# A fused two-block kernel on one core: product operands first in memory, modulations as rows, a second set of banks for the up products, and chains moved by a few ticks

## The chip, the cores and the metric

The kernel runs on one core of one Trainium2 chip. The metric is the time of one execution in microseconds on the device. The program on this core is five instruction streams, one for each engine: PE (TensorE, the matrix products), ACT (ScalarE, activations), DVE (VectorE, elementwise work), POOL (GpSimd) and SP (SyncE, which here only issues transfers). Each runs its own rows in order and meets the others at semaphores.

## The reference, cut to what matters

The reference runs two transformer blocks over 512 tokens of width 1024 (T = 4 tiles of 128 tokens), in float32. Block 1 is modulated by a vector c:

```python
ada = silu(c) @ w_ada + b_ada            # 6 groups of 1024: shift, gain, gate, twice
h = rmsnorm(x, n1) * (1 + gain1) + shift1
z = h @ w_in                             # q, k, v, index q and k, retention q, k, v, gate, ...
x = x + gate1 * (mix(sparse_attention(z), retention(z)) @ w_out)
h = rmsnorm(x, n2) * (1 + gain2) + shift2
x = x + gate2 * ((silu(h @ w_gate) * (h @ w_up)) @ w_down)     # 2816 wide
```

Block 2 has a rmsnorm, an attention with a compressed, a selected and a sliding branch (keys ks and kw, queries nq), a gated linear attention (decays from a small product gl, then exp and ln), and a feed-forward block whose two up products pass through a causal 3-tap convolution. The index scores choose the 256 keys that each query sees, so products have to be near full precision.

## The kernel before

**Products.** Every large product is made of three fp32r matmuls: an operand v is kept as a rounded high part and the rest, and hi·hi, hi·lo and lo·hi are added in one bank (`mm3`). A stationary operand of 128x128 meets up to 512 moving columns. The normed tokens lie in `Hh` and `Hl` (8 slices of 128 features by 512 tokens). Weights come in chunks of 128x1024 (512 KB) into `raw`, ACT writes their high part into `wh` (L1150), DVE the low part into `wl` (L1644). In the two down products, and in the projections after attention, the arrays `Ah` and `Al` serve too: as more places for weight chunks, or as the low and high part of the attention's output. `EH` and `EL` take the last slices of the second block's activation.

**Memory.** All arrays are allocated one after another in each partition, in the order of the allocation lines. Before, the order is X, Hh, Hl, raw, wh, wl, AR (a scratch arena), CST (tables), PRMT (parameters), BC, G, EH/EL (the same place as ACC), MC, ST, Ah/Al (the same place as AF). In bytes of a partition X begins at 16.5 KB, Hh and Hl lie at 33 to 66 KB, raw at 66 to 82, wh at 82 to 98, wl at 98 to 115, EH and EL at 199 to 207, and Ah and Al at 209 to 226.

**Order of the work.** `Weave` is a clock of ticks. A tick is the matmuls of one product step; all five programs walk through the same list of ticks. `w.after(n, f)` places f n ticks later in an engine's stream, `w.beside(generator)` advances a generator by one `yield` at each tick. Both only fix the place of small work between the dense matmuls in each engine's order; when it runs is left to the semaphores. `claim(b)` waits until the reader of PSUM bank b has freed it (there are 8).

**The start.** The stage iq multiplies the modulated, normed tokens with the index weights, feature slice by feature slice (k = 0 to 7). So slice k of the modulation has to be there before slice k of the product: silu(c) @ w_ada for 128 features of shift and 128 of gain. `LAND` takes the w_ada slices (1 MB each, 8 x 256 columns). DVE multiplies seven of eight row groups with silu(c) and adds them into two parts in G (`modulate`, L1659 and L1663); PE sums over the partitions with matmuls of one column (`modulation`, L526: CST,G and ST,AR). ACT then makes the modulated slice (L1204, L1205), DVE its low part. `norm_turn` is the transposes of the normed tokens (L535).

**The up products.** For a group j of 4 banks, the products of gate and up (m = 0 to 3) are made in banks 0 to 3, in each group the same four. ACT (silu, L1418) or, in block 2, ACT and DVE (the convolution, L1663) read them out. `down` uses all 8 banks for 4 tiles x 2 halves.

**The second attention.** In the stage 2nq, queries come tile by tile. Each tile's chain is: ACT copy and square, DVE head sums (L1666), POOL root, DVE scaling, gain and rotation (L1656), then the transposes on PE (`turn_heads`). `decays` makes the linear attention's decay factors beside it: 4 small products, DVE, then exp and ln on ACT (L1523, each with an ACT_TABLE_LOAD). `compressed` makes the compressed keys; it needs a gelu on ACT (L1488), whose result PE transposes. `attention` then runs score rows (DVE L1937), softmax, transposes and values between the product ticks. `linear` runs later, beside the output projection.

Of the kernel before, what the change touches and what calls it, by code (L numbers as in the profile page):

```python
# [114 lines left out]
NR, NH, NP = 4, 4, 8  # L115
# [194 lines left out]
def program(nc, x_in, cst_in, prm_in, bc_in, brow_in, wst, out):  # L310
# [12 lines left out]
    with ctx:  # L323
# [11 lines left out]
        wl = sb("wl", [P, NH, 1024], f32r)  # L335
        AR = sb("AR", [P, 13952])
# [4 lines left out]

        with nc.sbuf_tensor("EH", [P, 2, S], f32r) as EH, nc.sbuf_tensor("EL", [P, 2, S], f32r) as EL:
            pass
        ACC = sb("ACC", [P, 2, D])
        MC = sb("MC", [P, 32])
        ST = sb("ST", [P, 640])

        with nc.sbuf_tensor("Ah", [P, 4, S], f32r) as Ah, nc.sbuf_tensor("Al", [P, 4, S], f32r) as Al:
            pass
        AF = sb("AF", [P, 8, S])  # L350
# [57 lines left out]
        PART = [[G[:, 512 * i + 256 * j:512 * i + 256 * j + 256] for j in (0, 1)] for i in (0, 1)]  # L408
# [86 lines left out]

        TURNED = {"ks": (6, 4), "kw": (6, 3)}
# [19 lines left out]
        def tensor_program(e, on):  # L516
# [91 lines left out]
            def norm_turn(tag, t):  # L608
                xn, _ = norm_rows(tag, t)
                on.wait_ge(*dve.of((tag, "rows", t)))  # L610
                for n, b in enumerate(norm_banks(tag, t)):
# [4 lines left out]
                    free[b] = (act.of((tag, "gained", t)), dve.of((tag, "gained", t)))[n]  # L616

            on.wait_ge(s_cst, 16)
            for t in range(T):
                norm_turn("n1", t)  # L620

            def modulation(k):

                b, part, land = 6 + k % 2, PART[k % 2], LAND[k % 4]
                on.wait_ge(*act.of(("silu c",)))
                on.wait_ge(*dve.of(("sum", k)))
                claim(b)
                for m in (0, 1):
                    o = bank[b][:, m:m + 1]
                    mm(o, part[0][:, tok(m)], C("ones", 0, 1), True, False)  # L630
                    mm(o, part[1][:, tok(m)], C("ones", 0, 1), False, False)
                    x = mm(o, land[:, 7, tok(m)], SC[:, 7:8], False, True)
                x.then_inc(*small.mark(("modulation", k)))
                free[b] = dve.of(("mod1", k))

            modulation(0)
            modulation(1)

# [4 lines left out]
            for k, t in w.steps("iq"):  # L643
# [14 lines left out]
                else:  # L658
# [4 lines left out]
                    if k + 2 < 8:  # L663
                        modulation(k + 2)
# [183 lines left out]
            def up(prefix, tag, freed, fourth=None):  # L848
                for j, a, c in w.steps(prefix):
# [8 lines left out]
                    for m in (0, 2, 1, 3):  # L858
                        if c == 0 and a == 0:
                            claim(m)  # L860
# [1749 lines left out]
```

## Time and profile before

| what | value |
|---|---|
| median of 3 runs | 1628.5 us (1625.9 to 1630.48) |
| profiled execution | 1628.07 us, of which the span 1626.3 us |
| PE busy | 1590.8 us, 98% of the span |
| PE weight loads / DVE / ACT busy | 78% / 54% / 38% |
| mean granted TensorE clock | 0.994 |

PE is busy nearly all the time, so a gain has to come from PE's own time: idle stretches that are waits for another engine, matmuls that take longer than others of their kind, stretches at half clock, or small matmuls that fall away. "Busy" counts the modelled ends of matmuls, which overlap; two matmuls in a row that start 0.227 us apart are each listed with 0.39 us. What a matmul costs is therefore read from the distance between starts. In rows of the timeline the number in brackets is the idle time ahead of a row, and the engine and line that released it.

### The profile page before, as it was taken

Reading aid. Unit: us, or ns where it says so; the run is one execution under the profiler, and the core shown is the slowest. Engines: PE = TensorE matmul, PEld = TensorE weight load, DVE = VectorE, ACT = ScalarE, POOL = GpSimd, SP = SyncE. Lnnn points to the kernel's source line nnn. Section 1 sums busy time; section 2 is a strip of 40 time slices with the busy share of each in tenths; the row PEclk is TensorE's granted clock in tenths of the full one; section 3 lists DMA queues with packets and bytes.
Section 4 is the critical chain, followed back from the end, with each engine's and each line's share of the span. In section 5 each row is a group of like instructions: output and inputs, shape, how many; then the busy total and the mean of one; then the engine's idle time right before and its main releaser. Section 6 shows DMA issues by size and latency. Waiting matters only on the chain.

```text
span 1626.3 us, 19784 instructions
## 1 busy us (share of the span) xinstructions
PE 1590.8 (98%) x8003; PEld 1268.0 (78%) x8003; DVE 881.5 (54%) x1628; ACT 614.2 (38%) x1069; POOL 43.8 (3%) x82
## 2 busy tenths in 40 slices
PE   6999999999999999999999999899999999999999
PEld 5877877678888888888888886666768888887887
DVE  6769785655375653232333655676457455555432
ACT  4443334542312432222322454466425334344320
POOL 1000000000000000000000101100000000000000
PEclk8999999999999999999999999999999999999999
DMA  7512121136245334322222151110113222222221
GB/s 299 198 65 103 53 75 69 53 129 246 104 168 168 104 131 155 104 91 101 86 99 99 34 188 47 39 53 14 40 53 116 91 104 91 88 85 100 104 78 52
DMA packets 44883, 165.76 MB, mean 102 GB/s; under 512 B 5108, under 2 KB 5236, under 8 KB 43640
## 3 DMA queue, kind: packets, MB, share of 16 engines
q1 hardware_dynamic: 44792, 164.50, 28.8%
q8 instruction: 63, 1.03, 0.3%
q14 instruction: 28, 0.23, 0.0%
HBM read 162.38 MB, written 2.10 MB: 101 GB/s over the span
## 4 chain that ended last, share of the span: by engine, by line
PE 91%; DVE 4%; ACT 2%; issue 1%; POOL 1%; DMA 0%; SPq 0%; DVEq 0%; ACTq 0%
PE bank L526 87%; PE bank L535 4%; DVE AR L1656 1%; DVE AR L1663 1%; DMA X<-in_x 0%; DVE wl L1644 0%; POOL ST L2420 0%; DVE X L1656 0%; ACT wh L1150 0%; ACT AR L1161 0%; ACT AR L1173 0%; DVE CST L1656 0%; POOL ST L2418 0%; DVE ST L1666 0%; DVE Hl L1656 0%
## 5 line engine op out<-in xcount | busy, mean ns | idle before, releaser
L526 PE MATMUL bank<-wh,Hh 128*128 128x512 f32 (+1 forms) x1008 | 408.8, 406 | 0.4 <-DVE wl L1644 0.4
L526 PE MATMUL bank<-wh,Hl 128*128 128x512 f32 (+1 forms) x1008 | 392.6, 390 | 0.0
L526 PE MATMUL bank<-wl,Hh 128*128 128x512 f32 (+1 forms) x1008 | 392.2, 389 | 0.0
L1150 ACT ACTIVATE wh<-raw 128x1024 fp32r<-128x1024 f32 (+2 forms) x195 | 203.6, 1047 | 403.6 <-PE bank L526 391.4
L1644 DVE TENSOR_TENSOR wl<-raw,wh 128x1024 fp32r<-128x1024 f32 (+2 forms) x195 | 234.3, 1209 | 138.9 <-ACT wh L1150 138.3
L526 PEld LDWEIGHTS bank<-wh,Hh 128*128 128x128 f32 x1008 | 190.5, 189 | 58.0 <-issue 21.7
L526 PEld LDWEIGHTS bank<-wh,Hl 128*128 128x128 f32 x1008 | 190.2, 189 | 40.5
L526 PEld LDWEIGHTS bank<-wl,Hh 128*128 128x128 f32 x1008 | 190.7, 189 | 34.3
L526 PE MATMUL bank<-Hh,wh 128*128 128x512 f32 (+2 forms) x504 | 190.5, 378 | 2.6 <-DVE AR L1663 1.2
L526 PE MATMUL bank<-Hh,wl 128*128 128x512 f32 (+2 forms) x504 | 189.4, 376 | 0.0
L526 PE MATMUL bank<-Hl,wh 128*128 128x512 f32 (+2 forms) x504 | 189.3, 376 | 0.0
L526 PEld LDWEIGHTS bank<-Hh,wh 128*128 128x128 f32 (+1 forms) x504 | 94.5, 187 | 21.3 <-issue 1.6
L1656 DVE TENSOR_TENSOR Hl<-AR,Hh 128x512 fp32r<-128x512 f32 x68 | 45.8, 690 | 116.0 <-ACT Hh L1429 112.9
L526 PEld LDWEIGHTS bank<-Hl,wh 128*128 128x128 f32 (+1 forms) x504 | 94.5, 187 | 17.6 <-issue 0.2
L526 PEld LDWEIGHTS bank<-Hh,wl 128*128 128x128 f32 (+1 forms) x504 | 94.5, 187 | 17.7
L535 PE MATMUL bank<-CST,AR 128*128 128x128 f32 (+1 forms) x545 | 89.2, 285 | 18.7 <-DVE AR L1659 12.3
L535 PEld LDWEIGHTS bank<-CST,AR 128*128 128x128 f32 (+1 forms) x545 | 66.3, 144 | 52.1 <-issue 10.3
L526 PE MATMUL bank<-Hh,Ah 128*128 128x512 f32 (+1 forms) x272 | 100.5, 370 | 0.5 <-DVE X L1656 0.5
L526 PE MATMUL bank<-Hh,Al 128*128 128x512 f32 (+1 forms) x272 | 100.1, 368 | 0.0
L526 PE MATMUL bank<-Hl,Ah 128*128 128x512 f32 (+1 forms) x272 | 100.0, 368 | 0.0
L1150 ACT ACTIVATE Ah<-raw 128x1024 fp32r<-128x1024 f32 x46 | 48.5, 1057 | 129.7 <-PE bank L526 128.0
L1663 DVE SCALAR_TENSOR_TENSOR AR<-bank,PRMT,AR 128x511 f32<-128x511 f32 x88 | 63.9, 746 | 56.7 <-ACT AR L1624 55.1
(245 smaller groups left out, 1878.5 us busy)
## 6 DMA issues: line engine op xcount, KB each, us to landing
raw<-in_wst SPq DMA_DIRECT2D x268, 512.0 KB, 3.6
AR<-in_wst SPq DMA_DIRECT2D x8, 1024.0 KB, 6.5
X<-in_x SPq DMA_DIRECT2D x8, 512.0 KB, 4.9
AR<-in_wst SPq DMA_DIRECT2D x5, 512.0 KB, 6.0
out<-X SPq DMA_DIRECT2D x8, 256.0 KB, 2.1
CST<-in_cst SPq DMA_DIRECT2D x1, 1619.0 KB, 9.6
raw<-in_wst SPq DMA_DIRECT2D x4, 296.0 KB, 2.8
BC<-in_bc SPq DMA_DIRECT2D x2, 512.0 KB, 6.9
```

Source lines behind the costliest of these rows:

```text
L526: return e.matmul(o, l, r, start=start, stop=stop, skip_group_check=True)
L535: return e.transpose(o, a, C("ident")[0:n, 0:n])
L1150: e.activation(HI[slot[i]][:, 0:width(i)], raw[:, i % NR, 0:width(i)], ACT.Copy).then_inc(*w_hi.mark(i))
L1644: e.tensor_tensor(LO[slot[i]][:, 0:n], raw[:, i % NR, 0:n], HI[slot[i]][:, 0:n].bitcast(f32), SUB).then_inc(*w_lo.mark(i))
L1656: return e.tensor_tensor(o, a, b, op).then_inc(*dve.mark(*events))
L1663: return e.scalar_tensor_tensor(out=o, in0=a, scalar=s, in1=b, op0=op0, op1=op1).then_inc(*dve.mark(*events))
```

## The change

Four things are changed; nothing of what is computed.

- The allocation order becomes Hh, Hl, wh, wl, Ah/Al, EH/EL (with ACC), X, raw, AR, CST, PRMT, BC, G, MC, ST. Hh is then at 16.5 to 33 KB, Hl up to 49, wh up to 66, wl up to 82, Ah and Al at 82 to 98, EH and EL up to 107; X, raw, AR, CST, PRMT, BC, G and ST lie higher than before, up to 226 KB.
- Modulation slices are made differently. `SCZ` holds silu(c) as a stationary operand of 32 columns, of which the first is silu(c) and 31 are zero. `modulation_rows` streams the w_ada slice past it: 8 matmuls of 256 columns, four of them into each of four groups of 32 output rows. DVE copies the rows to SBUF (`MROW`), and `modulation_columns` sums them with 2 matmuls of one column. Slices 4, 6 and 7 (`ADDED`) are instead summed on DVE, all eight groups into one row. The x tiles come ahead of the first w_ada slice in SP's queue, both halves of the last token tile are copied out by ACT, and the full-precision slice (`FUL`) of slices 0 and 1 is made by DVE.
- `up_bank` puts group j's four products in banks 0 to 3 or 4 to 7 in turn, and the first down step takes tiles 2 and 3 first.
- In block 2, `decays` starts two ticks sooner on three engines, and waits correspondingly longer before its second part, whose banks alternate; the compressed keys use bank 7 for 6; the last two query tiles' scaling and transposes come later (10 and 13 or 14 ticks instead of 4 and 7); `linear` passes one tick between its sums and its scaling.

```diff
-        X = sb("X", [P, T, D])
         Hh = sb("Hh", [P, 8, S], f32r)
         Hl = sb("Hl", [P, 8, S], f32r)
-        raw = sb("raw", [P, NR, 1024])
         wh = sb("wh", [P, NH, 1024], f32r)
         wl = sb("wl", [P, NH, 1024], f32r)
+        with nc.sbuf_tensor("Ah", [P, 4, S], f32r) as Ah, nc.sbuf_tensor("Al", [P, 4, S], f32r) as Al:
+            pass
+        AF = sb("AF", [P, 8, S])
...
+        X = sb("X", [P, T, D])
+        raw = sb("raw", [P, NR, 1024])
         AR = sb("AR", [P, 13952])
...
+        ADDED = (4, 6, 7)
+        def mod_bank(k):
+            return 5 + k % 3 if k else 0
+        def up_bank(j, m):
+            return m + 4 * (j % 2)
...
+            def modulation_rows(k):
+                b = mod_bank(k)
+                on.wait_ge(*dve.of(("spread",)))
+                on.wait_ge(s_pre[k % 4], 16 * (k // 4 + 1))
                 claim(b)
+                for q in range(8):
+                    r = slice(32 * (q % 4), 32 * (q % 4) + 32)
+                    x = mm(bank[b][r, 0:256], SCZ[:, q, :], LAND[k % 4][:, q, :], q < 4, q >= 4)
+                x.then_inc(*small.mark(("mod rows", k)))
+            def modulation_columns(k):
+                b = mod_bank(k)
+                on.wait_ge(*dve.of(("mod rows", k)))
                 for m in (0, 1):
+                    x = mm(bank[b][:, 256 + m:257 + m], MROW[k % 2][:, tok(m)], C("ones", 0, 1), True, True)
...
                     if k + 2 < 8:
-                        modulation(k + 2)
+                        modulation_columns(k + 2)
+                if (k, t) == (0, 0):
+                    modulation_columns(1)
+                if t == 2 and k + 2 < 8 and k + 2 not in ADDED:
+                    modulation_rows(k + 2)
...
+                    tiles = ((2, 3, 0, 1) if k == 0 else range(T)) if t is None else (t,)
...
             def decays():
-                for _ in range(3):
-                    yield
+                yield
...
-                    lambda t: w.after(7, lambda: turn_heads("nq", t, 2, TN[t], dve.of(("nq", "roped", t)))), 2)
+                    lambda t: w.after((7, 7, 13, 14)[t], lambda: turn_heads("nq", t, 2, TN[t], dve.of(("nq", "roped", t)))), 2)
...
-                    w.after(2, root)
-                    w.after(4, scale)
+                    w.after((2, 2, 2, 4)[t], root)
+                    w.after((4, 4, 10, 10)[t], scale)
...
+                    yield
                     on.wait_ge(*pool.of(("lroot", t)))
...
+            load_x(0)
             e.dma_start(PRMT[:, 0:now], prm_in[:, 0:now]).then_inc(s_prm, 16)
             e.dma_start(CST[:, 0:early], cst_in[:, 0:early]).then_inc(s_cst, 16)
-            load_x(0)
-            load_x(1)
+            for t in range(1, T):
+                load_x(t)
             land(0)
-            load_x(2)
-            load_x(3)
```

**PE at the very start.** Before, PE's stream opens with the transposes of all four token tiles (32), then modulation slices 0 and 1, each as two triples of one-column matmuls (G holds DVE's sums, ST silu(c), AR the w_ada slice), then the dense matmuls.

```order
L535 MATMUL bank<-CST,AR 128x128 x32
L526 MATMUL bank<-CST,G 128x1 x2
L526 MATMUL bank<-ST,AR 128x1
L526 MATMUL bank<-CST,G 128x1 x2
L526 MATMUL bank<-ST,AR 128x1
L526 MATMUL bank<-CST,G 128x1 x2
L526 MATMUL bank<-ST,AR 128x1
L526 MATMUL bank<-CST,G 128x1 x2
L526 MATMUL bank<-ST,AR 128x1
L526 MATMUL bank<-wh,Hh 128x512
L526 MATMUL bank<-wl,Hh 128x512
```

After the change, the same place reads as follows (G is now the copied rows, ST the widened silu(c)).

```order
L548 MATMUL bank<-CST,AR 128x128 x24
L539 MATMUL bank<-AR,ST 32x256 x8
L548 MATMUL bank<-CST,AR 128x128 x8
L539 MATMUL bank<-CST,G 128x1 x2
L539 MATMUL bank<-AR,ST 32x256 x8
L539 MATMUL bank<-wh,Hh 128x512
L539 MATMUL bank<-wl,Hh 128x512
L539 MATMUL bank<-wh,Hl 128x512
L539 MATMUL bank<-CST,G 128x1 x2
L539 MATMUL bank<-wh,Hh 128x512
L539 MATMUL bank<-wl,Hh 128x512
L539 MATMUL bank<-wh,Hl 128x512
```

Eight transposes moved behind the first group of row matmuls, a second group stands ahead of the first dense matmul, slice 1's one-column matmuls moved behind three dense ones, and each slice has 2 of these where there were 6.

**ACT in the stage 2nq.** L1541 and L1543 are the copy and square of a query tile, L1523 exp and ln of the decays (with their table loads), L1463 copies of the kw keys' transposes, L1488 the gelu of the compressed keys. Before:

```order
L1541 ACTIVATE AR<-bank 128x512
L1543 ACTIVATE AR<-AR 128x512
L1541 ACTIVATE AR<-bank 128x512
L1543 ACTIVATE AR<-AR 128x512
L1523 ACT_TABLE_LOAD
L1523 ACTIVATE AR<-AR 128x256 x4
L1463 ACTIVATE AR<-bank 128x2x256 x2
L1523 ACT_TABLE_LOAD
L1523 ACTIVATE AR<-AR,CST 128x256 x4
L1488 ACT_TABLE_LOAD
L1488 ACTIVATE AR<-bank 128x256
```

After:

```order
L1572 ACTIVATE AR<-bank 128x512
L1574 ACTIVATE AR<-AR 128x512
L1552 ACT_TABLE_LOAD
L1552 ACTIVATE AR<-AR 128x256 x4
L1552 ACT_TABLE_LOAD
L1552 ACTIVATE AR<-AR,CST 128x256 x4
L1572 ACTIVATE AR<-bank 128x512
L1574 ACTIVATE AR<-AR 128x512
L1493 ACTIVATE AR<-bank 128x2x256 x2
L1518 ACT_TABLE_LOAD
L1518 ACTIVATE AR<-bank 128x256
```

The exp, the ln and their two table loads moved ahead of the second tile's copy and square; between the last of these and gelu only two key copies and the gelu's own table load are left.

**DVE around the first score rows of the second attention.** A score row is a pair of ISA rows. The chain of a query tile's scaling is the five rows from `AR<-AR,ST 128x512` to `AR<-ST 128x8x16`. Before, tile 2's chain stands ahead of the first score row, and tile 3's right behind it:

```order
L1656 TENSOR_TENSOR AR<-AR,ST 128x512
L1656 TENSOR_TENSOR AR<-AR,PRMT 128x512
L1656 TENSOR_TENSOR ST<-AR,CST 128x128
L1656 TENSOR_TENSOR ST<-AR,CST 128x8x8 x2
L1656 TENSOR_TENSOR AR<-ST 128x8x16
L1666 TENSOR_REDUCE ST<-AR 128x8
L1644 TENSOR_TENSOR wl<-raw,wh 128x1024
L1937 ISA AR,ST<-bank,CST 128x128
L1937 ISA ST 128x1
L1937 ISA AR,ST<-bank,CST 128x128
L1937 ISA ST 128x1
L1656 TENSOR_TENSOR AR<-AR,ST 128x512
```

After, no such chain stands there; tile 2's stands behind the fifth score row, ahead of the division for an earlier row's softmax:

```order
L2001 ISA AR,ST<-bank,CST 128x128
L2001 ISA ST 128x1
L2001 ISA AR,ST<-bank,CST 128x128
L2001 ISA ST 128x1
L1692 TENSOR_TENSOR AR<-AR,ST 128x512
L1692 TENSOR_TENSOR AR<-AR,PRMT 128x512
L1692 TENSOR_TENSOR ST<-AR,CST 128x128
L1692 TENSOR_TENSOR ST<-AR,CST 128x8x8 x2
L1692 TENSOR_TENSOR AR<-ST 128x8x16
L1708 RECIPROCAL ST<-ST 128x2
L1695 TENSOR_SCALAR AR<-AR,ST 128x128 x2
```

Each of the two chains moved behind several score rows; the rows of a chain are the same.

## Rows read from the trace of the kernel before

**Rows 1.** The page: busy time of each engine, share of the span, instructions.

```profile
PE 1590.8 (98%) x8003; PEld 1268.0 (78%) x8003; DVE 881.5 (54%) x1628; ACT 614.2 (38%) x1069; POOL 43.8 (3%) x82
```

**Rows 2.** Waits of PE by releaser: us in total, times, longest us.

```profile
PE bank L535 <- ACT AR L1488: 3.1, 1, 3.1
...
PE bank L526 <- DVE AR L1663: 2.5, 3, 1.3
...
PE bank L526 <- DVE ST L1937: 2.1, 2, 1.5
PE bank L535 <- DVE PRMT L1669: 1.8, 1, 1.8
...
PE bank L535 <- DVE AR L1656: 1.5, 1, 1.5
```

**Rows 3.** Timeline of PE, the start: start us, duration us, operation, records, idle before.

```profile
16.25 1.72 PE L535 MATMUL bank<-CST,AR 128*128 128x128 f32 x8 [0.42 <-DVE AR L1659]
...
23.40 1.01 PE L526 MATMUL bank<-CST,G 128*128 128x1 f32 x4 [2.88 <-DVE G L1663]
...
25.98 0.77 PE L526 MATMUL bank<-wh,Hh 128*128 128x512 f32 x1
...
31.46 0.50 PE L526 MATMUL bank<-CST,G 128*128 128x1 f32 x4
...
32.72 0.48 PE L526 MATMUL bank<-wh,Hh 128*128 128x512 f32 x1
```

**Rows 4.** Timeline of the start, ACT and DVE.

```profile
12.73 1.04 ACT L1161 ACTIVATE AR<-X 128x1024 f32<-128x1024 f32 x1
...
21.28 2.06 DVE L1663 SCALAR_TENSOR_TENSOR G<-AR,ST,G 128x256 f32<-128x256 f32 x5
```

**Rows 5.** Windows: stretch, us, PE busy (records), granted clock, DMA share, GB/s.

```profile
16.55:30.20 13.65, 10.77 (x42) 0.50 0.88 346
1003.00:1006.40 3.40, 2.84 (x8) 0.50 0.00 0
1033.70:1037.10 3.40, 3.40 (x14) 0.50 0.02 5
```

**Rows 6.** Timeline of PE in the first down product, Ah, then wh.

```profile
606.64 0.40 PE L526 MATMUL bank<-Hh,Ah 128*128 128x512 f32 x1
...
617.80 0.39 PE L526 MATMUL bank<-Hh,wh 128*128 128x512 f32 x1
...
628.00 0.39 PE L526 MATMUL bank<-Hh,wh 128*128 128x512 f32 x1
```

**Rows 7.** PE by line and shape: operands (moving, stationary), count, busy, mean, idle.

```profile
L526 PE MATMUL bank<-wh,Hh 128*128 128x512 f32 x976 | 398.3, 408 | 0.4 <-DVE wl L1644 0.4
...
L526 PE MATMUL bank<-Hh,wh 128*128 128x512 f32 x432 | 168.9, 391 | 1.6 <-DVE AR L1663 1.2 <-ACT AR L1418 0.4
...
L526 PE MATMUL bank<-Hh,Ah 128*128 128x512 f32 x208 | 82.2, 395 | 0.0
...
L526 PE MATMUL bank<-Ah,Hh 128*128 128x512 f32 x112 | 44.4, 397 | 0.0
...
L526 PE MATMUL bank<-wh,Ah 128*128 128x512 f32 x64 | 26.8, 418 | 0.0
```

**Rows 8.** Timeline of PE: two matmuls of 64 outputs each, the next.

```profile
996.87 0.65 PE L526 MATMUL bank<-AR,CST 128*64 128x256 f32 x4
997.46 0.50 PE L526 MATMUL bank<-wh,Hh 128*128 128x512 f32 x1
```

**Rows 9.** Timeline of ACT: the gelu of the compressed keys.

```profile
1003.12 0.38 ACT L1488 ACTIVATE AR<-bank 128x256 f32<-128x256 f32 x1
```

**Rows 10.** Timeline of DVE: a query tile's scaling, first and last step; the division.

```profile
1027.87 0.69 DVE L1656 TENSOR_TENSOR AR<-AR,ST 128x512 f32<-128x512 f32 x1 [1.46 <-POOL ST L2420]
...
1029.92 0.29 DVE L1656 TENSOR_TENSOR AR<-ST 128x128 f32<-128x128 f32 x1
...
1042.10 0.17 DVE L1672 RECIPROCAL ST<-ST 128x2 f32<-128x2 f32 x1 [0.66 <-ACT AR L1318]
```

More of the change, by code:

```diff
@@ L1017, in decays @@
                     yield
-                for _ in range(3):
+                for _ in range(5):
                     yield
@@ L1208, in scalar_program @@
                 norm_root("n1", t, (s_in[t], 16))
-                if t:
-                    rows_out(t - 1)
-            rows_out(T - 1)
+            for t in range(T):
+                if t == 3:
+                    split_high(place["iq", 0])
+                rows_out(t)
             split_high(place["ik", 0])
-            split_high(place["iq", 0])
             features(0)
@@ L1515, in decays @@
             def decays():
-                for _ in range(3):
-                    yield
+                yield
                 for t in range(T):
@@ L1632, in vector_program @@
         def vector_program(e, on):
+            early = set()
             def consume(i):
+                if i in early:
+                    return
+                early.add(i)
                 key, k, n = chunks[i][0], chunks[i][1], width(i)
@@ L1715, in modulated, with modulation_rows @@
-            def modulated(k):
-                b = bank[6 + k % 2]
-                on.wait_ge(*small.of(("modulation", k)))
-                tt(MC[:, k:k + 1], b[:, 0:1], W("b01", k, 1), ADD)
-                stt(MC[:, 8 + k:9 + k], b[:, 1:2], W("b01", 8 + k, 1), W("n1", k, 1), ADD, MUL, ("mod1", k))
+            def modulation_rows(k):
+                on.wait_ge(*small.of(("mod rows", k)))
+                if k >= 2:
+                    on.wait_ge(*small.of(("modulation", k - 2)))
+                copy(MROW[k % 2], bank[mod_bank(k)][:, 0:256], ("mod rows", k))
@@ new lines, in modulated, with modulation_sums @@
+            def modulated(k):
+                b = bank[mod_bank(k)]
+                on.wait_ge(*small.of(("modulation", k)))
+                tt(MC[:, k:k + 1], b[:, 256:257], W("b01", k, 1), ADD)
+                stt(MC[:, 8 + k:9 + k], b[:, 257:258], W("b01", 8 + k, 1), W("n1", k, 1), ADD, MUL, ("mod1", k))
+            def modulation_sums(k):
+                land, row = LAND[k % 4], MROW[k % 2]
+                on.wait_ge(s_pre[k % 4], 16 * (k // 4 + 1))
+                on.wait_ge(*small.of(("modulation", k - 2)))
+                ts(row, land[:, 0, :], SC[:, 0:1], None, MUL, None)
+                for q in range(1, 8):
+                    own()
+                    stt(row, land[:, q, :], SC[:, q:q + 1], row, MUL, ADD, *[("mod rows", k)] * (q == 7))
+                    if q in (1, 3, 5, 6, 7):
+                        yield
@@ L1721, in features_low, with added_rows, features @@
+            def added_rows():
+                for k, tick in zip(ADDED, (8, 16, 22)):
+                    while w.k < tick:
+                        yield
+                    yield from modulation_sums(k)
+            def features(k):
+                own()
+                on.wait_ge(*act.of(("n1", "gained", T - 1)))
+                ts(FUL[k % 2], AF[:, k, :], MC[:, 8 + k:9 + k], MC[:, k:k + 1], MUL, ADD)
             def features_low(k):
+                own()
                 on.wait_ge(*act.of(("n1", "high", k)))
@@ L1745, in vector_program @@
             ts(W("b01", 8, 8), W("b01", 8, 8), 1.0, None, ADD, None)
+            e.memset(SCZ, 0.0).then_inc(*dve.mark())
+            own()
+            on.wait_ge(*act.of(("silu c",)))
+            copy(SCZ[:, :, 0], SC, ("spread",))
             open_sum(2)
@@ L2245, in decays @@
             def decays():
-                for _ in range(3):
-                    yield
+                yield
                 for t in range(T):
@@ L2492, in sync_program @@
             for k in range(4):
-                on.wait_ge(*small.of(("modulation", k)))
+                on.wait_ge(*small.of(("mod rows", k)))
                 land(k + 4)
```

149 lines of the change are left out of this document (73 added, 76 removed).

## The prediction

> **What bounds the kernel now.** I read the busy times on the page first: PE is busy for 98% of the span, DVE for 54%, ACT for 38% [rows 1]. The reader is to see that no other engine can be the limit on average, and that all a change can win lies in PE's own stream. So the next views are those of PE: what it waits for [rows 2], the start [rows 3], the stretches at half clock [rows 5], and the distance between the starts of equal matmuls [rows 6]. Three kinds of loss come out of them.
>
> The start: the first dense matmul begins at 25.98 us [rows 3]. Ahead of it PE stands still for 2.88 us for DVE's modulation sums, and then spends 2.58 us (23.40 to 25.98) on slice 1's one-column matmuls.
>
> Waits in the stream: 3.1 us for the gelu, 1.8 and 2.1 us where the second attention opens, 1.5 us once in the output projection, and 2.5 us for PSUM banks of the up products [rows 2], with 0.4 us more for silu [rows 7]. Two of them are followed by a stretch of 3.4 us at a granted clock of 0.50, half of the full speed of 2.4 GHz; each comes after PE stood still [rows 5].
>
> A slow operand: in the first down product, 48 matmuls with a chunk in Ah and Al take from 606.64 to 617.80, 11.16 us or 232.5 ns each; the 45 after them, with a chunk in wh and wl, take until 628.00, 226.7 ns each [rows 6]. Work, shapes and clock are the same; what differs is where the operand lies (Ah and Al are above 209 KB, wh and wl at 82 to 115 KB).
>
> **The change part by part.** Sums are against the profiled execution, 1628.07 us (1.8 us around the span of 1626.3); the median of the runs is 0.4 us above it, which I leave out.
>
> *Memory.* Matmuls of 512 columns with an Ah or Al operand: 208, 112 and 64, each of three products, so 1152 [rows 7]. At 5.8 ns each that is 6.7 us, if the new place (82 to 98 KB) treats them as it treats wh, which lies in it today. Bounds: nothing, and 6.7 us. I take 6.7, since the same shapes run at 226.7 ns there. The small matmuls' operands (AR, CST, G, ST) and X go higher; no row shows them at two heights, and their effect I put at 0.
> The Trainium skill, "SBUF — State Buffer", section "SBUF: two separate sides", says that PE and ACT have ports of their own and never wait on anyone; it knows no dependence on the address. By that rule the memory part would give 0, which is rival 1. The 5.8 ns of this trace speak against it, but they show a difference, not its cause.
>
> *Start.* Before, the last x tile's square ran at 12.73 [rows 4], behind 1 MB of w_ada in the queue. At the 346 GB/s of [rows 5] that megabyte takes 3.0 us, so the last tile comes about 3 us sooner and the first w_ada slice lands about when the tile did, near 12.9. Then PE does the first group of row matmuls. The nearest row is a pair of matmuls with 256 columns in two groups of 64 outputs, 0.59 us from start to start [rows 8] (4 records, since a float32 matmul leaves two). Eight matmuls in four groups of 32: if four run side by side, two rounds, 1.2 us; if only two do, 2.4 us; if none does, 4.7 us. I take 1.6 us at full clock, nearer to the low end because the pair in rows 8 plainly shares its time, and 3.2 us at half clock, which this stretch has [rows 5]. 12.9 + 3.2 gives 16.1; the last tile's transposes follow (16.25 to about 17.7 before) and end at 17.7. The copies out, the gain, the slice's high and low part then take about what the idle stretch of 2.88 us held [rows 3]: first dense matmul at 20.6, so 5.4 us sooner. DVE's sums for a slice (five steps 2.06 us, [rows 4]) are gone from this path; slice 1's group of rows lies inside those 2.9 us. Bounds: 18.5 (LAND early, four at once) and 24.
>
> *In the stream of iq.* Before, six slices cost 1.26 us each (31.46 to 32.72, 12 records, [rows 3]), 7.6 us. After, seven have 4 such records, 0.42 us, 2.9 us together, and slices 2, 3 and 5 have a group of rows of 1.6 us, 4.8 us. Together 7.7 us: a loss of 0.1, with bounds of a gain of 1.1 (groups of 1.2) and a loss of 9.4 (groups of 4.7). Slices 4, 6 and 7 go to DVE, 8 steps of 0.41 us each (2.06 over five, [rows 4]), spread over three or more ticks each; they hide behind the dense matmuls. Without that cover each would delay one slice by some 3 us.
>
> *Banks.* The 2.5 us of waits for the convolution (three of them, [rows 2]) and 0.4 us for silu [rows 7] go, since a group's banks have been free for a whole group: 2.9 us. What is late next is nothing: between groups PE already runs at the even distance.
>
> *Second block.* (a) The gelu waited on ACT behind exp, ln and their table loads and ran at 1003.12 [rows 9]; PE had been idle for its result for 3.1 us [rows 2]. The order shows exp and ln ahead of the second tile's copy. They come two ticks (24 dense matmuls at 0.227 us) or 5.4 us sooner, and let a copy and a square in, about 1.2 us. Exp needs the logits, which PE and DVE make two ticks sooner as well. The gelu then comes near 999, before PE asks (near 1000.5): all of the 3.1 us. (b) The two stretches at half clock vanish with their waits: PE was busy 2.84 and 3.40 us in them, half of that is 3.1 us; I take 2.8, since the small matmuls in them gain less. (c) Where the second attention opens, waits of 2.1 us (two, for score rows) and 1.8 us (for a copy) stood behind the two tiles' scaling chains on DVE: all 3.9 us. (d) In `linear`, two DVE operations of about 0.6 us leave the chain that ended in a wait of 1.5 us: 1.2 us. (e) The two chains come back later. One is 2.34 us of DVE (1027.87 to 1030.21) and enters ahead of a division that had 0.66 us of idle time before it [rows 10]: each can hold back the softmax's division, and with it PE's transposes, by up to 1.7 us; at least by nothing, if PE asks later. I take 1.2 us each, 2.4 us. Sum: 3.1 + 2.8 + 3.9 + 1.2 - 2.4 = 8.6 us.
>
> **Sum.** 6.7 + 5.4 - 0.1 + 2.9 + 8.6 = 23.5 us; 1628.07 - 23.5 = 1604.6 us.
>
> **Rivals.**
>
> 1. *The place in memory is not the cause.* Ah and Al could be slow for what is written or read beside them. Against: rows 6 are one stage with one pattern, and all shapes with Ah show it. For: one example of each height. The part gives 0: 1611.3 us.
> 2. *Row matmuls run two at a time.* 0.8 us more for each of three groups in the stream, 1.6 us for each of two at the start at half clock: 5.6 us, 1610.2 us.
> 3. *The moved chains stall the attention.* Full 1.7 us each (1.0 us more), and PE's idle time there brings one stretch at half clock back (1.7 us) and a second wait behind it (1 us): 1608.3 us.
> 4. *The group of rows runs one matmul after another.* 3.1 us more for each of three, 6.2 us for each of two: 21.7 us, 1626.3 us, no change that can be told. The pair in rows 8 speaks against it.
> 5. *Slower.* The distance depends on the place in another way than by height, and the operands' new places (Hh, Hl, wh and wl all move) are ones where it is 232.5 ns. In this kernel 4224 matmuls of 512 columns have neither Ah nor Al (976 and 432 of two kinds, each of three products, [rows 7]). At 5.8 ns they lose 24.5 us, and the 6.7 us don't come: 1635.8 us. It decides from 4.0 ns each (16.8 us of other gains over 4224). Against it: Hl and wh go where Hh and Hl run evenly today; only the places of X and raw, which Hh and wl take, are untried.
>
> That the change doesn't do what it says is possible for the banks alone (a group's reader might be later than a whole group); it is worth at most 2.9 us and lies in the range.
>
> **How the numbers follow.** Chances: forecast 0.52 (its own range 1598 to 1609: the chains free of cost, 2.4, and a start at 18.5, 2.1, below; a start at 23 and chains at 1.7 above), rival 1 0.19, rival 2 0.10, rival 3 0.11, rival 4 0.04, rival 5 0.04. The first four lie below 1612; two of them together (1 and 2, 1617) are rare. Range: 1597 to 1615 us. A measurement of this kernel tells 0.3%, 4.9 us, from no change. Faster: 0.52 + 0.19 + 0.10 + 0.11 = 0.92; the same: 0.04 (rival 4); slower: 0.04 (rival 5).
>
> **What would show it.** Memory: the distance in the down product is 227 ns in every chunk. Start: the first dense matmul near 20.6; a group of row matmuls (16 records) takes 1.2 to 1.6 us at full clock. Banks: no wait of PE for L1418's or L1663's successors between groups. Second block: no wait for the gelu, no stretch at 0.50 behind 1000 us, and small waits of about 1.2 us for the division's result or for score rows further on in the attention. The prediction is wrong if dense matmuls run at 232 ns anywhere in a stage with no small work, if a group of rows takes over 2.5 us, or if new waits of PE add up to more than 5 us.

## The result, and the profile after

The changed kernel takes 1603.93 us (median of 4 runs, 1602.26 to 1605.5), against 1628.88 us for the kernel before (4 runs). The ratio is 0.9849, with a 95% interval of 0.9829 to 0.9868: 24.95 us faster. The prediction was 1604.6 us, with a range of 1597 to 1615. The profiled execution took 1602.26 us, with a span of 1600.4 us.

PE's line of the page (before: [rows 1]): PE is still busy for 98% of a shorter span, with 14.8 us less work.

```profile
PE 1576.0 (98%) x8019; PEld 1257.9 (79%) x8019; DVE 875.0 (55%) x1604; ACT 613.2 (38%) x1068; POOL 44.3 (3%) x82
```

**Where the time came from.** Both kernels issue the same 5976 dense matmuls in the same order, so the start of the same matmul in both timelines shows what has been gained up to there. Before, three of them:

```profile
51.92 0.47 PE L526 MATMUL bank<-wh,Hh 128*128 128x512 f32 x1
...
880.99 0.39 PE L526 MATMUL bank<-Ah,Hh 128*128 128x512 f32 x1
...
1229.94 0.40 PE L526 MATMUL bank<-wl,Hh 128*128 128x512 f32 x1
```

After, the same three:

```profile
43.07 0.47 PE L539 MATMUL bank<-wh,Hh 128*128 128x512 f32 x1
...
868.29 0.39 PE L539 MATMUL bank<-Ah,Hh 128*128 128x512 f32 x1
...
1210.59 0.39 PE L539 MATMUL bank<-wl,Hh 128*128 128x512 f32 x1
```

With the first dense matmul (25.98 in [rows 3], 18.71 below) and the two spans this gives the gain up to each place:

| up to | before | after | gained |
|---|---|---|---|
| first dense matmul | 25.98 | 18.71 | 7.3 |
| near the end of iq | 51.92 | 43.07 | 8.9 |
| down product of block 1, past its half | 880.99 | 868.29 | 12.7 |
| second attention and half of the output projection | 1229.94 | 1210.59 | 19.4 |
| end | 1626.3 | 1600.4 | 25.9 |

**The start** answers to [rows 3]. PE's timeline, with the idle time ahead of a row in brackets:

```profile
13.38 1.40 PE L539 MATMUL bank<-AR,ST 128*32 128x256 f32 x16
14.72 1.09 PE L548 MATMUL bank<-CST,AR 128*128 128x128 f32 x8
15.65 0.50 PE L539 MATMUL bank<-CST,G 128*128 128x1 f32 x4
16.64 1.07 PE L539 MATMUL bank<-AR,ST 128*32 128x256 f32 x16 [0.49 <-ACT AF L1223]
18.71 0.47 PE L539 MATMUL bank<-wh,Hh 128*128 128x512 f32 x1 [1.00 <-DVE Hl L1692]
19.01 0.39 PE L539 MATMUL bank<-wl,Hh 128*128 128x512 f32 x1
...
19.48 0.50 PE L539 MATMUL bank<-CST,G 128*128 128x1 f32 x4
...
21.40 1.07 PE L539 MATMUL bank<-AR,ST 128*32 128x256 f32 x16
22.40 0.50 PE L539 MATMUL bank<-wh,Hh 128*128 128x512 f32 x1
...
23.89 0.50 PE L539 MATMUL bank<-CST,G 128*128 128x1 f32 x4
24.26 0.48 PE L539 MATMUL bank<-wh,Hh 128*128 128x512 f32 x1
```

The 16 records of a group of row matmuls take 1.00 us from start to start (21.40 to 22.40) at full clock. That is less than the 1.2 us that two rounds of four would take by [rows 8], so the eight matmuls run four at a time. The second dense matmul starts 0.3 us after the first, and the two slices' one-column matmuls cost 0.36 and 0.37 us (19.48 to 19.84 and 23.89 to 24.26). The first dense matmul waited 1.00 us for DVE's low part. All of this ran at full clock: dense matmuls follow each other every 0.23 us, and the windows say the same (columns as in [rows 5]):

```profile
16.00:30.00 14.00, 12.51 (x95) 1.00 1.02 418
1014.00:1024.00 10.00, 9.90 (x59) 1.00 0.01 2
1028.20:1031.70 3.50, 3.50 (x16) 0.56 0.00 0
```

The third window holds a stretch at 0.50 (its mean is 0.56, since it reaches a little beyond the stretch), in the second attention, where PE never stood still for more than 0.42 us in the 14 us before it.

**An Ah chunk** answers to [rows 6]: 48 matmuls in 10.88 us, 226.7 ns each; then 45 in wh in 10.20 us, 226.7 ns each. One correction: the stretch at 606 us, which the heading of [rows 6], the prediction and the expectations call the first down product, belongs to the up products of block 1. ACT goes on reading their banks for silu until 804.80 us before the change, and the down product follows. Ah chunks serve in both stages, in the up products as the stationary and in the down products as the moving operand, and nothing else in the argument hangs on the name.

```profile
596.31 0.39 PE L539 MATMUL bank<-Hh,Ah 128*128 128x512 f32 x1
...
607.19 0.39 PE L539 MATMUL bank<-Hh,wh 128*128 128x512 f32 x1
...
617.39 0.39 PE L539 MATMUL bank<-Hh,wh 128*128 128x512 f32 x1
```

**Waits of PE** (columns as in [rows 2]). The convolution's and silu's waits are gone, the gelu's too. What took 2.5 us is new.

```profile
PE bank L539 <- DVE AR L1692: 3.4, 4, 1.1
PE bank L548 <- DVE AR L1705: 2.5, 1, 2.5
...
PE bank L539 <- DVE ST L2001: 0.2, 1, 0.2
...
PE bank L548 <- DVE AR L1692: 0.3, 1, 0.3
```

### The profile page after: what moved, and what is told of

It is laid out like the page before. It is cut to its first block, busy times and chain, and to the rows that moved or that the text cites. A ratio compares the mean times of both kernels' runs of the same rounds, so it can differ in the third digit from the quotient of the medians.

```text
span 1600.4 us, 19799 instructions
## 1 busy us (share of the span) xinstructions
PE 1576.0 (98%) x8019; PEld 1257.9 (79%) x8019; DVE 875.0 (55%) x1604; ACT 613.2 (38%) x1068; POOL 44.3 (3%) x82
## 4 chain that ended last, share of the span: by engine, by line
PE 92%; DVE 5%; ACT 2%; issue 1%; POOL 1%; DMA 0%; SPq 0%; DVEq 0%; ACTq 0%
PE bank L539 87%; PE bank L548 4%; DVE AR L1692 1%; DVE wl L1680 1%; POOL ST L2483 0%; DVE G L1699 0%; DVE X L1692 0%; DVE Hl L1692 0%; ACT wh L1176 0%; ACT AR L1199 0%; DVE CST L1692 0%; ACT AR L1187 0%; DMA CST<-in_cst 0%; DVE ST L1702 0%; DVE AR L1699 0%
## 5 line engine op out<-in xcount | busy, mean ns | idle before, releaser
L1176 ACT ACTIVATE wh<-raw 128x1024 fp32r<-128x1024 f32 (+1 forms) x195 | 203.6, 1047 | 398.2 <-PE bank L539 386.2
L1680 DVE TENSOR_TENSOR wl<-raw,wh 128x1024 fp32r<-128x1024 f32 (+1 forms) x195 | 234.2, 1208 | 137.1 <-ACT wh L1176 136.1
```

The source lines that it names most:

```text
L1176: e.activation(HI[slot[i]][:, 0:width(i)], raw[:, i % NR, 0:width(i)], ACT.Copy).then_inc(*w_hi.mark(i))
L1680: e.tensor_tensor(LO[slot[i]][:, 0:n], raw[:, i % NR, 0:n], HI[slot[i]][:, 0:n].bitcast(f32), SUB).then_inc(*w_lo.mark(i))
```

## The experiments

Each kernel was timed beside the kernel before on the same chip; its medians there were 1629.11, 1629.25 and 1628.54 us. Twelve kernels ran, in three groups. Where one is set against the changed kernel (1603.93 us), the two were timed on different occasions; those differences carry the spread of both, some 2 us. The traces allow a finer comparison, since the dense matmuls come in the same order in all fourteen kernels.

### One part at a time

Each of the first four is the kernel before with one part of the change.

`mem_only` has the allocation order alone:

```diff
-        X = sb("X", [P, T, D])
         Hh = sb("Hh", [P, 8, S], f32r)
...
+        with nc.sbuf_tensor("Ah", [P, 4, S], f32r) as Ah, nc.sbuf_tensor("Al", [P, 4, S], f32r) as Al:
```

> The kernel before with nothing changed but the order of the allocations. Theory (the place of Ah and Al costs 5.8 ns for each of 1152 matmuls of 512 columns): 6.7 us faster than before, near 1622, and 227 ns from start to start in all chunks of the down product. Rival (the place is nothing to a matmul, as the Trainium skill has it in "SBUF — State Buffer", section "SBUF: two separate sides"): no change, 1628.9, and the gain of these stages in the changed kernel came from its other edits.

`start_only` has `modulation_rows`, `modulation_columns`, `ADDED`, DVE's features of slices 0 and 1, and the order of transfers:

```diff
-                        modulation(k + 2)
+                        modulation_columns(k + 2)
```

> The kernel before with only the start's edits (modulation rows, the x tiles first, three slices summed on DVE). From the distance between equal dense matmuls of the two traces, these edits should give 8.9 us, 7.3 of them before the first dense matmul: near 1620. The prediction had 5.3 us for them; it would be right if the full clock in the changed kernel's start is owed to another edit, and then the granted clock is 0.50 again ahead of the first dense matmul and the run is near 1623.5.

`banks_only` has `up_bank` and the order of tiles in the first down step:

```diff
+            return m + 4 * (j % 2)
```

> The kernel before with only the second set of banks for the up products and the order of tiles in the first down step. Theory: the four waits (0.37, 0.66, 0.59 and 1.26 us) go, with the restart behind each 3.5 us, near 1625.4, and no new wait in the up products. Rival (the wait moves to the next reader of the banks): under 1 us.

`second_only` has the edits of `decays`, bank 7, the query tiles' ticks and the tick in `linear`:

```diff
-                    w.after(4, scale)
+                    w.after((4, 4, 10, 10)[t], scale)
```

> The kernel before with only the second block's edits (decays two ticks sooner, query tiles' scaling and transposes later, the tick in the linear attention). From the two traces these give 6.5 us net, near 1622.4: 11 us of waits and half clock removed, and 2.5 us (transposes of a query tile behind a copy on DVE), 1.0 us (linear attention's second tile) and about 1.9 us (a stretch at half clock) new. The prediction had 8.6 us. If the stretch at half clock doesn't come back in this kernel, it is 8.4 us, near 1620.5.

| part | predicted gain | median (range, runs) | gain | ratio, 95% interval |
|---|---|---|---|---|
| memory | 6.7 | 1622.64 (1622.27 to 1624.69, 5) | 6.5 | 0.9965, 0.9953 to 0.9977 |
| start | 5.3 | 1621.57 (1620.86 to 1624.02, 5) | 7.5 | 0.9959, 0.9947 to 0.9971 |
| banks | 2.9 | 1624.79 (1622.3 to 1625.68, 7) | 4.3 | 0.9975, 0.9965 to 0.9985 |
| second block | 8.6 | 1623.62 (1620.93 to 1626.55, 7) | 5.5 | 0.9972, 0.9961 to 0.9983 |
| sum | 23.5 | | 23.8 | |

The four gains add up to 23.8 us, the whole change gave 24.95: the parts don't depend on each other within what these runs can tell (each interval is about 1.0 to 1.2 thousandths, some 2 us, to either side). The memory part's gain is there with nothing else changed.

**The clock at the start.** `start_only` ran at half clock behind its first dense matmul, though its start is that of the changed kernel. In `second_only`, whose start is that of before with its idle 2.88 us, the record of the granted clock shows full clock throughout. Their windows:

```profile
18.80:25.30 6.50, 6.36 (x29) 0.50 1.01 413
```

```profile
16.55:30.20 13.65, 10.77 (x43) 1.00 0.87 336
1000.00:1040.00 40.00, 36.45 (x243) 1.00 0.16 53
```

But in the first of the two windows of `second_only` the matmuls contradict that record. They start 0.43 us apart, as in the kernel before at 0.50, where full clock gives 0.23 us:

```profile
27.07 0.63 PE L527 MATMUL bank<-wl,Hh 128*128 128x512 f32 x1
27.50 0.63 PE L527 MATMUL bank<-wh,Hl 128*128 128x512 f32 x1
```

So the start of `second_only` ran at half pace too, and the distance between starts is what to trust. Read by it, the fourteen profiles of this case fall into two groups at the first dense matmuls. "Idle" is PE's last wait ahead of them. The kernels of the table that were not named yet come further down.

| profiles | last idle ahead of the first dense matmul | dense matmuls behind it |
|---|---|---|
| the changed kernel, `ah_64`, `fixed` | 0.99 to 1.00 us | 0.23 us apart |
| `ah_32`, `rows_all`, `w_out_of_step`, `start_only` | 1.69 to 1.97 us | 0.43 us apart for some us |
| `start_late` | 5.62 us | 0.43 us apart |
| the kernel before and the five others with its start | 2.87 to 2.88 us | 0.43 us apart |

The new start makes the short idle time possible, but doesn't ensure it. In the five profiles of the new start at half pace ACT had waited 0.57 to 1.17 us for the transfer of the second weight chunk, behind which it makes the slice that PE needs; in the three at full pace it had not. `ah_32`, `rows_all` and `w_out_of_step` hold all four parts of the change, so the full clock isn't owed to one of the other parts either: the expectation for `start_only` had left that open. By the distance between equal dense matmuls the half pace cost `start_only` 2.9 us against the changed kernel up to the end of iq. That the idle time is the cause is the simplest reading of the table; no run sets it alone between 1.00 and 1.69 us.

The spread of the runs of one kernel goes with the mean granted clock: the four of the changed kernel took 1602.26 and 1602.44 us at 0.999 and 1605.41 and 1605.5 at 0.997.

### What makes an operand slow

`mem_only` confirmed the gain, not the reason. The next run took the opposite order: all operands of the dense products last, above everything else.

```diff
-        Hh = sb("Hh", [P, 8, S], f32r)
...
         ST = sb("ST", [P, 640])
+        Hh = sb("Hh", [P, 8, S], f32r)
+        Hl = sb("Hl", [P, 8, S], f32r)
...
+        wh = sb("wh", [P, NH, 1024], f32r)
+        wl = sb("wl", [P, NH, 1024], f32r)
```

> The kernel before with all product operands allocated last, in the order Hh, Hl, EH and EL, Ah and Al, wh, wl, so that they span about 129 to 226 KB. Theory (a product with an operand above some height costs 5.8 ns more): in the down product chunks in wh and wl, now at about 193 to 226 KB, run at 232.5 ns too, and Ah and Al stay slow or not according to where the bound lies. If all products are slow: 4224 x 5.8 ns, 24.5 us slower than before, near 1653.5. Rival (Ah and Al are slow for themselves, not for their place): no change.

Measured: 1623.11 us (1622.06 to 1624.89, 7 runs), ratio 0.9964 (0.9952 to 0.9975). Neither expectation came true: it is 6.1 us faster than before, the same gain as with all operands low. The same Ah chunk in this kernel, 48 matmuls in 10.88 us:

```profile
606.33 0.39 PE L526 MATMUL bank<-Hh,Ah 128*128 128x512 f32 x1
...
617.21 0.39 PE L526 MATMUL bank<-Hh,wh 128*128 128x512 f32 x1
```

That refutes the height: Hh begins at 135,680 bytes here, Ah at 176,640, wl at 209,408, which is the very place that Ah had before. What the even cases share shows in the addresses modulo 256 bytes:

| kernel | Hh, Hl, wh, wl | EH, EL | Ah, Al | Ah chunks |
|---|---|---|---|---|
| before | 128 | 128 | 0 | 232.5 ns |
| after, `mem_only` | 128 | 128 | 128 | 226.7 ns |
| `operands_high` | 0 | 0 | 0 | 226.7 ns |

(MC, of 128 bytes, lies between EH and Ah before, and shifts Ah.) So the new theory: a matmul is slow when its two operands lie at different places modulo 256. Four runs tested it, and they bore it out, but for one kind of chunk in `ah_64`, which cost less than the others. The first leaves all arrays of the kernel before where they are, and moves Ah by 128 bytes:

```diff
+        PAD = sb("PAD", [P, 32])
         with nc.sbuf_tensor("Ah", [P, 4, S], f32r) as Ah, nc.sbuf_tensor("Al", [P, 4, S], f32r) as Al:
```

> The kernel before with 128 bytes left free ahead of Ah, and nothing else. Ah begins at 209536 in place of 209408: as high as before, but its place modulo 256 bytes is 128, as that of Hh, Hl, wh, wl and EH. Theory (a matmul is slow when its two operands differ in their place modulo 256 bytes): all of the memory part's gain, 6.5 us, near 1622.7, and 227 ns in all chunks of the down product. Rival (the run with all operands high was even for another reason, such as the distance between operands and scratch): no change.

Measured: 1622.92 us (1621.65 to 1623.49, 5 runs), ratio 0.9965 (0.9951 to 0.9978), 5.6 us faster than the 1628.54 beside it. The Ah chunk takes 10.88 us for its 48 matmuls, 226.7 ns each:

```profile
606.30 0.39 PE L527 MATMUL bank<-Hh,Ah 128*128 128x512 f32 x1
...
617.18 0.39 PE L527 MATMUL bank<-Hh,wh 128*128 128x512 f32 x1
```

The second does the reverse in the changed kernel, and to wh and wl:

```diff
+        PAD = sb("PAD", [P, 32])
         wh = sb("wh", [P, NH, 1024], f32r)
         wl = sb("wl", [P, NH, 1024], f32r)
+        PAD2 = sb("PAD2", [P, 32])
```

> The changed kernel with 128 bytes left free ahead of wh, and again ahead of Ah, so that wh and wl alone lie at 0 modulo 256 and all other operands at 128, all of them below 107 KB. Theory: the down product's chunks change roles, 227 ns in Ah and 232 ns in wh, and 4224 matmuls with wh or wl get 5.8 ns longer: 24.5 us slower, near 1628.5. Rival (only Ah can be slow): no change, 1604.

Measured: 1624.93 us (1621.11 to 1629.02, 10 runs), 21.0 us slower than the changed kernel; the profiled execution's span is 1625.7 us, 25.3 us longer than the changed kernel's. The chunks have changed roles. The Ah chunk takes 10.88 us for 48 matmuls, the 44 matmuls after it in wh 10.24 us, 232.7 ns each. The 24.5 us expected were too many for what followed: summed over all groups with wh or wl as one operand (now 4464 matmuls, with those against Ah and EH), PE's busy time grew by 21.7 us, since a matmul with wh or wl as the moving operand got only 4 to 5 ns longer in the mean. In the profiled execution a first dense matmul 0.6 us later, and some 2.5 us of half clock behind it, come on top.

```profile
606.95 0.39 PE L541 MATMUL bank<-Hh,Ah 128*128 128x512 f32 x1
...
617.83 0.40 PE L541 MATMUL bank<-Hh,wh 128*128 128x512 f32 x1
...
628.07 0.39 PE L541 MATMUL bank<-Hh,wl 128*128 128x512 f32 x1
```

The last two leave 64 and 32 bytes ahead of Ah in the changed kernel (a PAD of 16 and of 8 elements).

> The changed kernel with 64 bytes left free ahead of Ah, so that Ah, Al, EH and EL lie at 192 modulo 256, Hh, Hl, wh and wl at 128. If any difference modulo 128 or 256 makes a matmul slow: 6.5 us slower, near 1610.5. If only the half of the 256 bytes counts (0 to 127 against 128 to 255): no change. If it is a matter of degree: some 3 us.

> The changed kernel with 32 bytes left free ahead of Ah (160 modulo 256). If any difference counts: 6.5 us slower. If only the half of the 256 bytes counts: no change. If it is a matter of degree: some 1.6 us.

Measured: 1610.86 us (1609.54 to 1612.31, 4 runs) and 1612.14 us (1611.45 to 1613.36, 4 runs), 6.9 and 8.2 us slower than the changed kernel. The Ah chunk in the up products takes 11.20 us for its 48 matmuls with 64 bytes (shown below), 233.3 ns each, and the same with 32 bytes (600.31 to 611.51 us):

```profile
597.30 0.40 PE L540 MATMUL bank<-Hh,Ah 128*128 128x512 f32 x1
...
608.50 0.39 PE L540 MATMUL bank<-Hh,wh 128*128 128x512 f32 x1
```

With Ah as the stationary operand a difference of 32, 64 or 128 bytes costs the same 6 ns or so: it is neither a matter of the half of the 256 bytes nor of degree. With Ah as the moving operand against Hh there is an exception. A chunk of 48 in the down product takes 233.2 ns each at a difference of 128 bytes (the kernel before), 233.4 at 32 bytes, but 229.2 at 64 bytes:

```profile
829.92 0.40 PE L540 MATMUL bank<-Ah,Hh 128*128 128x512 f32 x1
...
840.92 0.40 PE L540 MATMUL bank<-wh,Hh 128*128 128x512 f32 x1
```

Why that one costs less is open. In the same kernels Ah against EH, both moved by the same pad, stays even (227.5 and 227.4 ns for 48 matmuls), which is what the theory says. A multiple of 256 costs nothing: EH before lay at 198,528, that is 384 modulo 512, against 128 for wh, and was even. And the matmuls of 256 columns show none of it: before, those with Ah start 121 ns apart in the mean, those with wh 122. Whether what counts is the two operands of one matmul, or a moving operand and the weights of the next matmul that are loaded meanwhile, these runs don't separate, since both differ together in a stream.

### The start

```diff
+            for _ in range(8):
+                own()
+                e.memset(FUL[1], 0.0).then_inc(*dve.mark())
             features(0)
```

> The changed kernel with eight fills of 128x512 on DVE (some 0.4 us each) ahead of the first slice's features, so that PE idles some 3.3 us more ahead of the first dense matmul. Theory (the full clock at the start is owed to the shorter idle time): the granted clock falls to 0.50 again, and the cost is 3.3 us and about 2 to 4 us of half clock behind it, near 1610. Rival (the clock is full there for another reason): only the 3.3 us, near 1607.

Measured: 1608.69 us (1608.03 to 1611.96, 4 runs), 4.8 us slower than the changed kernel. The first dense matmul came 4.85 us later (the fills cost more than I had put on them), and in the profiled execution half clock followed:

```profile
16.87 1.07 PE L539 MATMUL bank<-AR,ST 128*32 128x256 f32 x16 [0.49 <-DMA AR<-in_wst]
23.56 0.76 PE L539 MATMUL bank<-wh,Hh 128*128 128x512 f32 x1 [5.62 <-DVE Hl L1692]
```

```profile
21.00:30.50 9.50, 6.94 (x30) 0.50 0.77 316
```

The profiled execution is the slowest of the four (1611.96 us at a mean clock of 0.995; the others 1608.03 to 1608.88 at 0.997 and 0.998, the changed kernel's own range of clocks being 0.997 to 0.999). The median cost is that of the delay. The half clock behind the longer idle time is what the theory said, and fits the table of the fourteen profiles above; the start of the other three executions was not recorded, so that it comes every time is not shown.

```diff
-        ADDED = (4, 6, 7)
+        ADDED = ()
```

> The changed kernel with slices 4, 6 and 7 of the modulation as row matmuls on PE too, none summed on DVE. A group of rows takes 1.00 us from start to start in the changed kernel's trace, so theory: 3.0 us slower, near 1607. Rival (DVE's sums delay something in the stage, so that taking them off DVE gives part back): under 1.5 us slower.

Measured: 1609.56 us (1607.69 to 1610.89, 4 runs), 5.6 us slower. By the distance between equal dense matmuls the three further groups cost 2.3 us in the profiled execution, a bit less than three times 1.00, since the same slices' sums leave DVE. The same execution lost 3.1 us to half clock in the start and more near 513 us, and the mean clocks of the four runs are 0.995 to 0.998. The half clock at the start follows an idle time of 1.85 us, where the changed kernel had 1.00. So DVE's three sums are worth at least the 2.3 us; what of the rest is theirs stays open.

### A version that beats both

The wait of 2.5 us that is new in the profile after stands in the second block. The timeline of ACT, PE and DVE around it, in order of time:

```profile
981.70 1.71 ACT L1552 ACTIVATE AR<-AR,CST 128x256 f32<-128x256 f32 x4
983.32 0.57 ACT L1572 ACTIVATE AR<-bank 128x512 f32<-128x512 f32 x1
...
986.84 0.38 ACT L1518 ACTIVATE AR<-bank 128x256 f32<-128x256 f32 x1
...
987.27 0.44 PE L548 MATMUL bank<-CST,AR 128*128 128x128 f32 x2
...
988.83 0.69 DVE L1692 TENSOR_TENSOR AR<-AR,ST 128x512 f32<-128x512 f32 x1 [2.11 <-POOL ST L2483]
...
991.08 0.41 DVE L1705 COPY AR<-bank 128x256 f32<-128x256 f32 x1
...
991.64 0.63 PE L548 MATMUL bank<-CST,AR 128*128 128x128 f32 x4 [2.54 <-DVE AR L1705]
```

The gelu came at 986.84 and PE's transposes of its result at 987.27, without a wait. Then PE stood still for 2.54 us ahead of the first query tile's transposes, which need bank 2. It is freed by DVE's copy at 991.08 (L1705), and that copy is queued behind the second query tile's scaling chain (from 988.83), which is itself late: ACT's exp, ln and table loads now stand ahead of that tile's copy, which ran at 983.32. A second new wait is in the linear attention, where the moved tick put a weight chunk's low part ahead of a scaling that PE waits for:

```profile
1175.46 0.71 PE L539 MATMUL bank<-AR 64*128 64x128 f32 x4 [1.01 <-DVE AR L1692]
```

Both can be taken away without giving back what the edits won:

```diff
-                    w.after((4, 4, 10, 10)[t], scale)
+                    w.after((4, 6, 10, 10)[t], scale)
...
-                    yield
+                    if t == T - 1:
+                        yield
                     on.wait_ge(*pool.of(("lroot", t)))
...
+                    if t < T - 1:
+                        yield
```

> The changed kernel, in which the second query tile's scaling comes 6 ticks after its product in place of 4, so that DVE copies the compressed keys' hidden values (which frees bank 2) ahead of it, and in which the linear attention waits a tick only at its last tile. Theory: the new waits of PE, 2.54 us for the first query tile's transposes and 1.01 us in the linear attention, go: 3.5 us faster than the changed kernel, near 1600.4. Rival (the chain of the second tile stands in another's way where it goes now): under 1.5 us.

Measured: 1597.86 us (1597.21 to 1599.25, 4 runs), ratio to the kernel before 0.981 (0.9795 to 0.9826), against 0.9849 for the changed kernel: 6.1 us faster. In its trace the query tile's transposes follow at 988.89, and the eight records in the linear attention are one unbroken group:

```profile
987.23 0.44 PE L548 MATMUL bank<-CST,AR 128*128 128x128 f32 x2
...
988.89 0.60 PE L548 MATMUL bank<-CST,AR 128*128 128x128 f32 x4
```

```profile
1169.56 1.52 PE L539 MATMUL bank<-AR 64*128 64x128 f32 x8
```

2.7 and 0.9 us of the gain are these two waits, by the distance between equal dense matmuls; about the 3.5 us of the theory. The profiled pair differs by 5.0 us, and another 1.4 us of that is the stretch at half clock near 1028 us, which isn't there: this profile shows no half clock before its last 1.3 us. Three of the four runs were at 1.000, where the changed kernel had 0.997 to 0.999. That the shorter waits keep the clock up is likely, but it is not separated here from chance.

## Why the prediction was right

The time was forecast to 0.7 us, which is better than its parts deserve. The start came out 2.2 us better than forecast and the banks 1.4 us, the second block 3.1 us worse; that these nearly cancel is luck.

**Memory: the size was right, the reason wrong.** 6.7 us predicted, 6.5 measured. The step that said "what differs is where the operand lies" compared one high and one low array, and took height for the cause. The runs put in its place: the two operands of a matmul have to lie at the same place modulo 256 bytes. It came out right because the new order lines up all operands. (It counted 1152 matmuls; 48 more, Ah against EH and EL, were slow too, 0.3 us.) Rival 1 (the place is not the cause) fell. Rival 5 (slower) was a real danger under another name: `w_out_of_step` is 21 us slower for 128 bytes ahead of wh. The rule of the Trainium skill, "SBUF — State Buffer", section "SBUF: two separate sides", that PE never waits on anyone, gave 0 for this part; the measurement decides against that use of it, though not against its words: they are about engines waiting for each other, and no run here shows that such a wait is what makes these matmuls longer.

**Start: 5.3 us predicted, 7.5 measured (8.9 in the profiled pair).** The term that was mis-sized is the first group of rows: I carried the 0.50 of [rows 5] over to it, and had 3.2 us, and 1.6 us for a group at full clock. It took 1.3 us (13.38 to 14.72), and a group in the stream 1.0 us. In none of the eight profiles with the new start did this group run at half clock (1.00 to 1.34 us); where half clock came, it came later, behind the first dense matmul. Rivals 2 and 4 (two at a time, or one) fell with that. The idle stretch behind it was forecast well: the first dense matmul came 4.0 us after the last transposes began, where I had 4.5.

**Banks: 2.9 us predicted, 4.3 measured.** All four waits went and none came in their place. I had counted the idle times alone; the restart behind a wait costs PE some 0.15 us more each, and the interval (2.4 to 5.7 us) covers the rest.

**Second block: 8.6 us predicted, 5.5 measured.** Steps (c) and (d) were right: the waits of 3.9 us at the opening of the attention are down to the 0.2 us of L2001, and the linear attention's 1.5 to 0.3. Step (e) was wrong in a good way: the two chains came back at no cost that shows: no wait of PE is new in the score rows. Step (a) failed in part. The gelu's wait went as forecast, but I asked only what it was queued behind, not what the tile that was passed over would now be late for: its chain held DVE when bank 2's copy was due, 2.5 us. Step (d) brought 1.0 us at another tile, which I hadn't looked at. And step (b) was too sure. All six profiles with the old second block have both stretches at half clock; of the eight with the new one two have two, four have one (the changed kernel's came at 1028 us, without a wait ahead of it) and two none. So a part of the 2.8 us came, and how much differs from one execution to the next. The new wait of 2.54 us shows the same: the four transposes behind it took 0.63 us in the changed kernel, `ah_64` and `second_only`, 0.78 and 0.93 us in `start_late` and `w_out_of_step`, and 1.09 us, half pace, in `rows_all` and `ah_32`:

```profile
998.77 1.09 PE L549 MATMUL bank<-CST,AR 128*128 128x128 f32 x4 [2.53 <-DVE AR L1706]
```

## What to carry to other kernels

When equal matmuls run at two speeds, compare their operands' addresses modulo 256 bytes; an odd small array between large ones (here MC, of 128 bytes) is enough to put them out of step, and a pad that makes up the difference mends it. When work is moved ahead of other work on one engine, follow the work that was passed over to its own readers, and to whatever is queued behind it on the next engine. And read a stretch at half clock from several executions, and from the distance between equal matmuls rather than from the record of the clock alone, before putting it into a sum.

## What the runs showed of the hardware

- A float32r matmul of 128x128 by 512 columns starts every 226.7 ns in a steady stream when both operands lie at the same place modulo 256 bytes, and every 232.4 to 233.4 ns when they differ by 32 or 128 bytes, whichever of the two is the stationary one. At a difference of 64 bytes it is 233.3 ns with Ah stationary and 229.2 ns with Ah moving against Hh. Height in the partition (16 to 226 KB) makes no difference, and matmuls of 256 columns show no such effect.
- Eight float32 matmuls with 32 stationary columns and 256 moving ones, in four groups of output rows, take 1.00 us together with the switch there and back, where two with 64 stationary columns take 0.59 us [rows 8].
- Behind the start's idle time, all three profiles with 0.99 to 1.00 us ran on at full pace, and all eleven with 1.69 us or more at half pace for some us. In the second attention, behind the same 2.54 us, three profiles ran on at full pace and four fell to half pace, two of them at once. 0.001 of mean granted clock goes with about 1.6 us of this kernel.
- The record of the granted clock can miss a stretch: `second_only`'s shows 1.00 where its dense matmuls start 0.43 us apart.
